# Last panel of the pooling output: latent rows first, context joins behind them, other banks and order at the heads' entry

## The chip, the cores and the metric

The kernel runs on one core of a Trainium2 chip. The metric is the device time of one execution, in microseconds: the median of three runs. Five engines work side by side, each on its own list of instructions in order: PE (matmuls), DVE (vector), ACT (activations), POOL (GpSimd) and SP, which here only issues DMAs. They meet at semaphores: an instruction waits until a counter has reached a value, and another engine's instruction raises it when it ends.

## The reference

Everything is float32. A first block (attention of three kinds and a feed-forward part with a short convolution) works on 256 tokens of width 2048. What the change touches lies in the second block, of two layers: a pooling layer on 256 latent and 256 context tokens, and a latent-attention layer (MLA) on both.

```python
for i in range(2):
    shift, scale, gate = jnp.split(jax.nn.silu(c) @ ada_w[i] + ada_b[i], 3, axis=-1)
    h_lat = rms_norm(x, pre_norm[i]) * (1 + scale[:, None]) + shift[:, None]
    shift_c, scale_c, gate_c = jnp.split(jax.nn.silu(c_ctx) @ ada_w[i] + ada_b[i], 3, axis=-1)
    h_ctx = rms_norm(ctx, pre_norm[i]) * (1 + scale_c) + shift_c
    if is_pool:      # i == 0
        y_lat = pool_branch(h_lat, ...)        # ends in (y * silu(gate)) @ pool_w_out
        y_ctx = pool_branch(h_ctx, ...)
    else:            # i == 1
        y_lat, y_ctx = mla_branch(h_lat, h_ctx, ...)    # begins with proj = h @ mla_w_in
    x = x + gate[:, None] * rms_norm(y_lat, post_norm[i])
    if i == 0:
        ctx = ctx + gate_c * rms_norm(y_ctx, post_norm[i])
```

So between the last matmul of `pool_w_out` and the first of `mla_w_in` lie, for the latent rows, the RMS norm of the output, the residual sum, a second RMS norm with scale and shift, and a transpose. The MLA layer then projects to low-rank queries and keys (`c_q`, `c_kv`), a rotary key part `k_r` and gates, and works on 16 heads.

## The kernel before

**Weights as a stream.** All weights pass through a ring of four slots (`RING`). One chunk is 256 rows of 512 (MLA input: 448) columns. SP loads it into `raw` (helper `load_chunk`), ACT rounds it to `hi` (L541, in `his`), DVE makes `lo = raw - hi` (L545, in `los`), and PE multiplies in three passes, hi x hi, hi x lo, lo x hi (`by_tokens`, L598), so that products keep nearly float32 precision. A slot of `raw` is free for the next load once its `lo` is made (`lo_split`), and `hi`/`lo` of a slot are free once PE has used them (`chunks_used`). SP, ACT, DVE and PE all walk the same list of chunks in order. In that list stand, between the weights, chunks of `ada_w` (adaLN weights of the second block), which DVE alone consumes: four multiply-adds on 128x512 (L568, L574). After eight such chunks PE turns the finished row into columns with 16 one-column matmuls (`turn_ada`, L647) and DVE takes them into `adat` (`take_ada`, L653). Where they stand is set by lists of numbers (`POOL_OUT_ORDER`, `MLA_IN_ORDER`).

**Pooling output.** `y` (512 tokens) times `pool_w_out`, in four panels of 512 columns, two to a turn (`pool_out_turn` on PE). A panel has eight chunks; each makes 24 matmuls: 2 row blocks x 4 token tiles (tiles 0 and 1 latent, 2 and 3 context, `TT = 2`, `NT = 4`) x 3 passes. Panels use PSUM banks 0-3 and 4-7 in turn. After a panel ACT squares each bank with a running sum (`yout_squares`, L1350), DVE multiplies each with the gates (`yout_gated`, L1706). After the last panel come the mean (`yout_mean_square`), a POOL power to -0.5 (`yout_roots`, L1087), and `yout_join` (L1722): residual plus normalised row, for the latent rows into `xres`, for the context rows into `yout`.

**Norm for the MLA layer.** Two `Norm` objects, `n_mla` for the latent and `n_mla_ctx` for the context rows: squares on ACT (`norm_squares`, L673), mean on DVE (L749), power on POOL (`norm_root`, L754), scaling on DVE (`norm_apply`, L759, into `xn4b`), then eight groups: four transposes on PE (`norm_turn`, L775, banks 4-7), scale and shift on ACT (`norm_hi`, L805), high and low part on DVE (`norm_shift_split`, L830 and L837) into `k4_hi` and `k4_lo`.

**MLA panels.** Seven panels of 448 columns in the order 0, 3, 1, 2, 4, 5, 6 (`MLA_ORDER`); "panel p" below counts in this order. Each has eight chunks of 12 matmuls for the latent tiles, in banks 0-1 or 2-3 by turns; panels 2 and 3 also compute context columns. The latent groups are turned among the first chunks of panel 0, the context groups among those of panel 1, and panel 2 needs all of the context's groups. ACT copies each finished panel to `proj_l` (L1397, `mla_taken`). Under panels 4 to 6 run the norms of `c_q` and `c_kv` and the rotary keys, turned into banks 4 and 5 (`kr_hi` on ACT, L1392; `kr_lo` on DVE, L1909).

**Heads.** Eight pairs of heads. Per pair: queries from two chunks (banks 0-1), keys (banks 2-3, L2296), turning of q (L2307, L2309), values (banks 2-3, L2319, copied by DVE to `v_sb`, L1868), scores (banks 4-7, L2330 and L2332), DVE's maxima, ACT's exponentials (L1416), transposes of the probabilities (L2339), rows (L2347). The first pair's queries to values stand ahead of the loop, with the transposing of the gate gains (`turn_gates`, L2226) before them; the silu of the gates (L1428) stands on ACT before the first exponential.

## Time and profile before

| | us |
|---|---|
| median of 3 runs | 2441.76 |
| lowest, highest run | 2439.11, 2446.45 |
| the profiled execution | 2439.29 |
| its span in the trace | 2437.5 |
| PE busy | 2336.4 (96%) |
| DVE busy | 1656.9 (68%) |
| ACT busy | 1041.2 (43%) |
| POOL busy | 76.2 (3%) |

The profiled execution is one run of its own; its trace starts and ends a little inside the measured time. Times "at 1896" are microseconds from the start of the span. A timeline row gives start, duration, engine, source line and instruction with its tiles; "x4" means four merged instructions, and square brackets hold the engine's idle time before it and what ended it. The clock is PE's, as a share of its full rate. An engine's share of busy time says little by itself: what counts is which wait ended last at a place where PE stood still.

### The profile page before, as it was taken

What the parts mean: (1) busy time and instruction counts of PE and PEld (TensorE: products, weight loads), DVE (VectorE), ACT (ScalarE), POOL (GpSimd) and SP (SyncE); (2) the same over time, 40 slices, a digit from 0 to 9 for tenths busy, and PEclk for the clock granted to TensorE, in tenths of its full rate; (3) what the DMA queues carried; (4) which work ended last, traced back from release to release, by engine and by line L of the source; (5) the groups of instructions that cost most, each with busy time, mean ns of one, the idle gap of its engine ahead of it and who ended that gap; (6) DMA issues with size and microseconds to landing.
All of it is one profiled execution on the core that took longest, in us unless ns stands there. A gap on an engine that the chain in (4) does not pass through costs nothing.

```text
span 2437.5 us, 32050 instructions
## 1 busy us (share of the span) xinstructions
PE 2336.4 (96%) x11221; PEld 1935.8 (79%) x11221; DVE 1656.9 (68%) x2401; ACT 1041.2 (43%) x1490; POOL 76.2 (3%) x112
## 2 busy tenths in 40 slices
PE   8999999999999999999969999999999699899997
PEld 6778778878877877778858888887788699799976
DVE  5378866687787786777748585756758666456544
ACT  5575654555555555333342222222222535443433
POOL 1022210000000000000000000000000000000000
PEclk9999999999999999999989999999999899999999
DMA  7956545666676766777735464645557256312243
GB/s 240 206 167 197 165 137 158 189 217 219 209 234 199 232 212 201 249 238 243 249 108 185 144 198 137 200 139 171 205 169 221 82 170 181 114 61 68 74 140 136
DMA packets 225516, 430.32 MB, mean 177 GB/s; under 512 B 13800, under 2 KB 38624, under 8 KB 224129
## 3 DMA queue, kind: packets, MB, share of 16 engines
q1 hardware_dynamic: 222112, 418.96, 55.2%
q10 hardware_dynamic: 2720, 9.83, 1.3%
q8 instruction: 63, 1.03, 0.2%
q14 instruction: 45, 0.36, 0.1%
q0 software_dynamic: 576, 0.14, 0.0%
HBM read 426.16 MB, written 2.72 MB: 176 GB/s over the span
## 4 chain that ended last, share of the span: by engine, by line
PE 63%; issue 19%; DVE 7%; DMA 6%; ACT 4%; DVEq 0%; POOL 0%; ACTq 0%; SPq 0%; POOLq 0%
PE ps L598 37%; PE ps L631 11%; PE ps L608 9%; DMA raw<-in_w_down 4%; DVE lo L545 2%; ACT hi L541 2%; DVE ada_acc L574 2%; PE ps L647 1%; DVE ustage L1630 1%; DMA raw<-in_w_in 1%; PE ps L2202 1%; PE ps L2127 0%; DMA poolm<-const_pool 0%; PE ps L1979 0%; PE ps L775 0%
## 5 line engine op out<-in xcount | busy, mean ns | idle before, releaser
L541 ACT ACTIVATE hi<-raw 128x1024 fp32r<-128x1024 f32 x604 | 635.3, 1059 | 1148.8 <-PE ps L598 536.2
L545 DVE TENSOR_TENSOR lo<-raw,hi 128x1024 fp32r<-128x1024 f32 x604 | 731.4, 1222 | 520.4 <-ACT hi L541 517.5
L574 DVE SCALAR_TENSOR_TENSOR ada_acc<-raw,csil,ada_acc 128x512 f32<-128x512 f32 x720 | 491.8, 746 | 2.5 <-DMA raw<-in_ada_w 2.3
L598 PE MATMUL ps<-hi,h_hi 128*128 128x512 f32 x960 | 383.2, 399 | 8.1 <-DVE lo L545 6.5
L598 PE MATMUL ps<-hi,h_lo 128*128 128x512 f32 x960 | 378.9, 395 | 0.0
L598 PE MATMUL ps<-lo,h_hi 128*128 128x512 f32 x960 | 378.7, 395 | 0.0
L598 PEld LDWEIGHTS ps<-hi,h_hi 128*128 128x128 f32 x960 | 180.8, 188 | 55.4 <-DVE lo L545 13.4
L598 PEld LDWEIGHTS ps<-hi,h_lo 128*128 128x128 f32 x960 | 180.7, 188 | 42.5
L598 PEld LDWEIGHTS ps<-lo,h_hi 128*128 128x128 f32 x960 | 180.9, 188 | 40.1
L598 PE MATMUL ps<-hi,g_hi 128*128 128x512 f32 x352 | 140.9, 400 | 6.6 <-DVE lo L545 6.3
L631 PE MATMUL ps<-hi,h_hi 128*128 128x512 f32 (+1 forms) x352 | 142.2, 404 | 2.9 <-DVE h_lo L736 2.9
L598 PE MATMUL ps<-lo,g_hi 128*128 128x512 f32 x352 | 139.1, 395 | 0.0
L598 PE MATMUL ps<-hi,g_lo 128*128 128x512 f32 x352 | 139.0, 395 | 0.0
L631 PE MATMUL ps<-hi,h_lo 128*128 128x512 f32 (+1 forms) x352 | 136.9, 389 | 0.0
L631 PE MATMUL ps<-lo,h_hi 128*128 128x512 f32 (+1 forms) x352 | 136.6, 388 | 0.0
L598 PE MATMUL ps<-hi,k_hi 128*128 128x448 f32 (+2 forms) x288 | 102.6, 356 | 1.1 <-DVE k_lo L837 0.6
L598 PE MATMUL ps<-hi,y_hi 128*128 128x512 f32 x256 | 102.6, 401 | 0.0
L608 PE MATMUL ps<-h_hi,hi 128*128 128x512 f32 x256 | 102.0, 398 | 0.0
L598 PE MATMUL ps<-hi,y_lo 128*128 128x512 f32 x256 | 101.9, 398 | 0.0
L598 PE MATMUL ps<-lo,y_hi 128*128 128x512 f32 x256 | 101.9, 398 | 0.0
L598 PE MATMUL ps<-hi,k_lo 128*128 128x448 f32 (+2 forms) x288 | 101.5, 353 | 0.0
L598 PE MATMUL ps<-lo,k_hi 128*128 128x448 f32 (+2 forms) x288 | 101.5, 352 | 0.0
(320 smaller groups left out, 3710.3 us busy)
## 6 DMA issues: line engine op xcount, KB each, us to landing
raw<-in_ada_w SPq DMA_DIRECT2D x192, 512.0 KB, 4.2
raw<-in_w_up SPq DMA_DIRECT2D x176, 512.0 KB, 4.5
raw<-in_w_down SPq DMA_DIRECT2D x88, 512.0 KB, 5.4
raw<-in_w_in SPq DMA_DIRECT2D x84, 512.0 KB, 4.5
raw<-in_pool_w_in SPq DMA_DIRECT2D x64, 512.0 KB, 4.1
raw<-in_mla_w_in SPq DMA_DIRECT2D x56, 448.0 KB, 4.1
raw<-in_w_out SPq DMA_DIRECT2D x32, 512.0 KB, 3.8
raw<-in_pool_w_out SPq DMA_DIRECT2D x32, 512.0 KB, 4.7
```

What stands on the lines that cost most here:

```text
L541: act.activation(hi[:, slot, :, :], raw[:, slot, :, :], ACT.Copy).then_inc(hi_split, 1 + ada)
L545: dve.tensor_tensor(lo[:, slot, :, :], raw[:, slot, :, :], hi[:, slot, :, :].bitcast(F32), ALU.subtract).then_inc(lo_split, 1)
L574: ins = dve.scalar_tensor_tensor(acc, raw[:, slot, k, :], csil[:, v, kt:kt + 1], acc, ALU.mult, ALU.add)
L598: mm = pe.matmul(ps[:, bank, 0:n], a[:, kt0 + k, tok * P:(tok + 1) * P], w[:, slot, k, col0:col0 + n], start=first and k == 0 and s == 0, ...
L608: mm = pe.matmul(ps[:, bank0 + n, :], w[:, slot, k, n * P:(n + 1) * P], a[:, kt0 + k, :], start=first and k == 0 and s == 0, stop=last and ...
L631: mm = pe.matmul(ps[:, PAIR * half + tok, 0:width], x, w[:, k, :], start=first and k == 0 and s == 0, stop=last and k == nk - 1 and s == 2)
L647: mm = pe.matmul(ps[:, bank, at:at + 1], acc, negones[:, 0:1], start=True, stop=True)
L1630: ins = dve.scalar_tensor_tensor(conv[which][:, m, back:SEQ], turned_u(m)[:, 0:SEQ - back], cols[:, bass.ds(ch + vec[0] * P + vec[1], 1)], ...
L2202: mm = pe.matmul(ps[:, m, s * SEQ + c0:(s + 1) * SEQ], u[:, TT * s + k, m * P:(m + 1) * P], poolm[:, bass.ds(n, 1), k, c0:].rearrange("p a ...
```

## The change

- **Pooling output.** The loop over the two turns is written out, each turn with its own list (`POOL_OUT_ORDERS`). The second turn carries one adaLN panel instead of two. In its last panel the first four chunks run as before for all four tiles; the last four run for tiles 0 and 1 alone, signal `lat_summed`, and then run again for tiles 2 and 3, which frees the slots.
- **Latent chain.** ACT squares and DVE gates tiles 0 and 1 alone; mean and power are made for these two; the latent rows are joined and normed. The splits of the first four MLA chunks stand one by one between the steps. The context's squares, products, mean, power and joins stand behind the latent groups, among splits of MLA chunks.
- **Norm.** `k4_hi` and `k4_lo` are tiles for latent and context apart. The latent groups turn in banks 4, 5, 0, 1; the squares are written to SBUF. The context groups turn at chunks 3 to 5 of panel 1 (before: 0 to 2).
- **MLA panels.** They start in banks 2-3 instead of 0-1. Two adaLN panels lie among their weights (16 chunks behind weights 15 to 35) instead of one (8 chunks behind 16 to 30).
- **Heads' entry.** The first queries need only the sixth copy of `proj_l`; `turn_gates` stands behind them; the first values go to banks 6-7; `kr_lo` and the gate gains are made in the last MLA panel; the first scores stand ahead of the loop, and each turn of the loop ends with the next pair's scores.

On DVE at the end of the pooling output, before the change (`yout` products, then mean and joins; `lo<-raw,hi` is a chunk's split):

```order
L653 TENSOR_SCALAR adat<-ps 128x8 [waits ada_turned]
L545 TENSOR_TENSOR lo<-raw,hi 128x1024 [waits hi_split]
L1706 TENSOR_TENSOR yout<-ps,gate_rows 128x512 [waits yout_squared0] x4
L1714 TENSOR_REDUCE ss<-panel_sums 128x4 [waits yout_squared0]
L1716 TENSOR_SCALAR ms<-ss 128x4 [waits yout_summed0]
L545 TENSOR_TENSOR lo<-raw,hi 128x1024 [waits hi_split]
L1683 TENSOR_TENSOR adat<-adat,cols 128x64 [waits ada_taken]
L1687 SCALAR_TENSOR_TENSOR hscale<-adat,cols 128x16 [waits ada_biased]
L1687 SCALAR_TENSOR_TENSOR hscale<-adat,cols 128x16
L1722 SCALAR_TENSOR_TENSOR xres<-yout,rstd,xres 128x2048 [waits yout_root0,yout_taken] x2
L1722 SCALAR_TENSOR_TENSOR yout<-yout,rstd,ctx_res 128x2048 [waits yout_root0,yout_taken,ctx_again]
L749 TENSOR_SCALAR ms<-ss 128x2 [waits norm_squared]
```

The same place on DVE after the change:

```order
L1714 TENSOR_TENSOR adat<-adat,cols 128x64 [waits ada_taken]
L1718 SCALAR_TENSOR_TENSOR hscale<-adat,cols 128x16 [waits ada_biased]
L1718 SCALAR_TENSOR_TENSOR hscale<-adat,cols 128x16
L1737 TENSOR_TENSOR yout<-ps,gate_rows 128x512 [waits yout_squared0] x2
L1745 TENSOR_REDUCE ss<-panel_sums 128x2 [waits yout_squared0]
L1747 TENSOR_SCALAR ms<-ss 128x2 [waits yout_summed0]
L1753 SCALAR_TENSOR_TENSOR xres<-yout,rstd,xres 128x2048 [waits yout_root0,yout_taken] x2
L549 TENSOR_TENSOR lo<-raw,hi 128x1024 [waits hi_split]
L761 TENSOR_SCALAR ms<-ss 128x2 [waits norm_squared]
L771 TENSOR_SCALAR xn4b<-xres,rstd 128x2048 [waits norm_root]
L771 TENSOR_SCALAR xn4b<-xres,rstd 128x2048
L549 TENSOR_TENSOR lo<-raw,hi 128x1024 [waits hi_split]
```

The scales moved ahead of the products, two products and both context joins left this place, and a split stands behind the joins and another behind the scaling.

On DVE at the heads' entry, before the change (`q_rope` is the last step of the rotary queries):

```order
L1854 TENSOR_TENSOR q_rope<-q_rope,q_swap 128x256 [waits q_swapped]
L545 TENSOR_TENSOR lo<-raw,hi 128x1024 [waits hi_split] x2
L1858 TENSOR_TENSOR kn_lo<-ps,kn_hi 128x1024 [waits kn_hi_done]
L1862 TENSOR_TENSOR qn_lo<-ps,qn_hi 128x512 [waits q_hi_done]
L1864 TENSOR_TENSOR qr_lo<-ps,qr_hi 128x256
L1868 COPY v_sb<-ps 128x1024 [waits chunks_used]
L545 TENSOR_TENSOR lo<-raw,hi 128x1024 [waits hi_split] x2
L1909 TENSOR_TENSOR kr_lo<-ps,kr_hi 128x1024 [waits kr_hi_done]
```

And in the last MLA panel on DVE after the change:

```order
L549 TENSOR_TENSOR lo<-raw,hi 128x1024 [waits hi_split] x5
L1881 TENSOR_TENSOR kr_lo<-ps,kr_hi 128x1024 [waits kr_hi_done]
L1726 TENSOR_TENSOR adat<-adat,cols 128x32 [waits ada_taken]
L1729 TENSOR_TENSOR hscale<-adat,cols 128x16 [waits ada_biased]
L1729 TENSOR_TENSOR hscale<-adat,cols 128x16
L549 TENSOR_TENSOR lo<-raw,hi 128x1024 [waits hi_split] x3
L1893 TENSOR_TENSOR q_swap<-ps,rope 128x4x16 [waits q_nope_ready,kr_turned]
```

`kr_lo` and the gate gains (`adat`, `hscale`) moved ahead of the last three splits of the MLA stream; before, `kr_lo` stood behind the copy of `v_sb` and two more splits.

The diff, cut to its core:

```diff
-POOL_OUT_ORDER = turn_order(2 * CH, evenly(2 * CH, 2 * CH))
+POOL_OUT_ORDERS = [turn_order(2 * CH, evenly(2 * CH, 2 * CH)), turn_order(2 * CH, [RING + 7 * m // CH for m in range(CH)])]
...
-MLA_PANELS, MLA_ADA = MLA_W // W_IN, 1
-MLA_IN_ORDER = turn_order(MLA_PANELS * CH, [2 * CH + 2 * m for m in range(CH)])
+MLA_PANELS, MLA_ADA = MLA_W // W_IN, 2
+MLA_IN_ORDER = turn_order(MLA_PANELS * CH, [2 * CH - 1 + 4 * m // 3 for m in range(2 * CH)])
...
-            yout_roots(0)
+            yout_roots(0, LAT)
             norm_root(pool, n_mla)
+            yout_roots(0, CTX)
             norm_root(pool, n_mla_ctx)
...
+                    if last:
+                        his(act, first, 0, 0, at + RING, end)
+                        act.wait_ge(lat_summed, 1)
+                        yout_squares(0, i * 2 + half, 4 * half, slice(0, TT))
...
+            his(act, C_MLA, 0, 0, 0, 1)
+            norm_squares(act, n_mla, lambda e, i: e.wait_ge(yout_added[0], i + 1), 0, lat_junk[:, :])
+            his(act, C_MLA, 0, 0, 1, 2)
             act.wait_ge(scales_ready, 4)
-            norm_hi(act, n_mla)
+            norm_hi(act, n_mla, {3: lambda: his(act, C_MLA, 0, 0, 2, 3), 5: lambda: his(act, C_MLA, 0, 0, 3, 4)})
+            yout_squares(0, D // W - 1, 4, slice(TT, NT))
...
             scales(1, V_PRE1)
-            for i in range(TT):
-                yout_join(0, i, xres[:, i, :], xres[:, i, :])
-            dve.wait_ge(ctx_again, 16)
-            yout_join(0, TT, yout[:, TT, :], ctx_res[:, 0, :])
+            yout_gated(0, D // W - 1, 4, slice(0, TT))
+            yout_mean_square(0, LAT)
+            for tok in range(TT):
+                yout_join(0, tok, xres[:, tok, :], xres[:, tok, :])
+            los(dve, C_MLA, 0, 0, 0, 1)
             norm_mean(dve, n_mla)
-            yout_join(0, TT + 1, yout[:, TT + 1, :], ctx_res[:, 1, :])
             norm_apply(dve, n_mla)
-            norm_shift_split(dve, n_mla)
+            los(dve, C_MLA, 0, 0, 1, 2)
+            norm_shift_split(dve, n_mla, {3: lambda: los(dve, C_MLA, 0, 0, 2, 3), 5: lambda: los(dve, C_MLA, 0, 0, 3, 4)})
...
             mla_los(0, 0, RING)
+            yout_gated(0, D // W - 1, 4, slice(TT, NT))
+            yout_mean_square(0, CTX)
+            dve.wait_ge(ctx_again, 16)
+            for m in range(TT):
+                mla_los(0, RING + m, RING + m + 1)
+                yout_join(0, TT + m, yout[:, TT + m, :], ctx_res[:, m, :])
+            mla_los(0, RING + TT, CH)
             norm_mean(dve, n_mla_ctx)
             norm_apply(dve, n_mla_ctx)
-            mla_los(0, RING, CH)
-            norm_shift_split(dve, n_mla_ctx)
+            mla_los(1, 0, 3)
+            norm_shift_split(dve, n_mla_ctx, {3: lambda: mla_los(1, 3, 4), 5: lambda: mla_los(1, 4, 5)})
...
-            mla_los(6, 0, CH)
+            mla_los(6, 0, RING + 1)
+            dve.wait_ge(kr_hi_done, 1)
+            dve.tensor_tensor(kr_lo[:, :, :], ps[:, 4:6, :], kr_hi[:, :, :].bitcast(F32), ALU.subtract).then_inc(kr_lo_done, 1)
             gate_gains(1, V_POST1)
+            mla_los(6, RING + 1, CH)
...
-            pair_v(0)
+            pair_v(0, 6)
             los(dve, C_HEADS, 0, 4, RING + 2, RING + 4)
-            dve.wait_ge(kr_hi_done, 1)
-            dve.tensor_tensor(kr_lo[:, :, :], ps[:, 4:6, :], kr_hi[:, :, :].bitcast(F32), ALU.subtract).then_inc(kr_lo_done, 1)
...
+                if last:
+                    for j in range(RING):
+                        before(CH + j)
+                        part(j, outs, True)
+                    for j in range(RING, CH):
+                        before(CH + j)
+                        mm = part(j, outs[0:TT], False)
+                    mm.then_inc(lat_summed, 1)
+                    for j in range(RING, CH):
+                        part(j, outs[TT:NT], True)
...
-                if p == 1:
-                    norm_ahead(pe, n_mla_ctx, j, False)
+                if p == 1 and j >= 3:
+                    norm_ahead(pe, n_mla_ctx, j - 3, False)
...
-                panel_by_tokens(pe, C_MLA, 0, MLA_IN_ORDER, p * CH, k4_hi, k4_lo, pair(p % 2) + ctx_too, W_IN,
+                panel_by_tokens(pe, C_MLA, 0, MLA_IN_ORDER, p * CH, k4_hi, k4_lo, pair(1 - p % 2) + ctx_too, W_IN,
...
+            pe.wait_ge(mla_taken, PAIR + len(MLA_ORDER) - 1)
+            pair_queries(0, C_HEADS, 0)
+            turn_gates(1, 7)
             pe.wait_ge(mla_taken, PAIR + len(MLA_ORDER))
-            turn_gates(1, 7)
-            pair_queries(0, C_HEADS, 0)
             pair_keys(0, 0)
             pair_keys(0, 1)
             pair_turn(0)
-            pair_values(0)
-            pe.wait_ge(gates_out, 2)
+            pair_values(0, 6)
             pe.wait_ge(kr_lo_done, 1)
+            pe.wait_ge(kn_lo_done, 1)
+            pair_scores(0, True)
+            pe.wait_ge(v_ready, FREE + 1)
             with pe.Fori(0, PAIRS - 1) as i:
-                pair_scores(i)
                 pair_queries(i + 1, C_HEADS + RING, i)
...
                 pair_columns(i)
-            pair_scores(PAIRS - 1)
+                pair_scores(i + 1)
```

## Rows read from the trace of the kernel before

**Rows 1.** Waits of PE, whole span: who waited for whom, total us, times, longest.

```profile
PE ps L775 <- DVE xn4b L759: 17.6, 2, 17.0
...
PE ps L598 <- DVE lo L545: 13.4, 21, 0.9
```

**Rows 2.** Timeline at the heads' entry: start, duration, engine, line, instruction; idle time before it.

```profile
2098.90 0.27 PE L2226 MATMUL ps<-ident,hscale 128*32 128x128 f32 x1 [2.95 <-DVE hscale L1698]
...
2112.97 0.39 PE L2319 MATMUL ps<-hi,ckv_hi 128*128 128x256 f32 x1 [1.72 <-DVE kn_lo L1858]
...
2120.94 3.69 ACT L1428 ACTIVATE proj_l<-proj_l 128x2048 f32<-128x2048 f32 x2
...
2122.39 1.22 DVE L1909 TENSOR_TENSOR kr_lo<-ps,kr_hi 128x1024 fp32r<-128x1024 f32 x1
...
2123.95 0.79 PE L2330 MATMUL ps<-kn_hi,qn_hi 128*128 128x512 f32 x1 [5.02 <-DVE kr_lo L1909]
...
2124.65 1.28 ACT L1416 ACT_TABLE_LOAD   x1
...
2132.28 0.34 PE L598 MATMUL ps<-hi,cq_hi 128*128 128x384 f32 x1
...
2136.49 1.03 PE L2339 MATMUL ps<-ident,mprobs 128*128 128x128 f32 x8
```

**Rows 3.** Timeline from the pooling output to the MLA panels, same columns.

```profile
1897.06 2.48 DVE L1706 TENSOR_TENSOR yout<-ps,gate_rows 128x512 f32<-128x512 f32 x4 [5.23 <-ACT yout L1350]
...
1899.74 1.22 DVE L545 TENSOR_TENSOR lo<-raw,hi 128x1024 fp32r<-128x1024 f32 x1
1899.90 1.93 POOL L1087 TENSOR_TENSOR rstd<-ms,halves 128x4 f32<-128x4 f32 x1 [658.22 <-DVE ms L1716]
...
1906.59 1.88 ACT L673 ACTIVATE ps<-xres 128x2048 f32<-128x2048 f32 x1 [0.26 <-DVE xres L1722]
...
1908.80 2.34 DVE L1722 SCALAR_TENSOR_TENSOR yout<-yout,rstd,ctx_res 128x2048 f32<-128x2048 f32 x1
1908.97 2.73 POOL L754 TENSOR_TENSOR rstd<-ms,halves 128x2 f32<-128x2 f32 x1 [7.15 <-DVE ms L749]
...
1918.32 0.47 PE L598 MATMUL ps<-hi,k_hi 128*128 128x448 f32 x1 [0.58 <-DVE k_lo L837]
```

**Rows 4.** Chain of waits, the end of PE's pooling output: start, duration, what.

```profile
1888.81 1.68 PE ps L647 x16
1890.49 5.70 PE ps L598 x24
```

**Rows 5.** Timeline of POOL: two powers with DVE waiting for them.

```profile
1231.17 0.69 POOL L754 TENSOR_TENSOR rstd<-ms,halves 128x2 f32<-128x2 f32 x1 [785.80 <-DVE ms L749]
...
1935.55 0.70 POOL L754 TENSOR_TENSOR rstd<-ms,halves 128x2 f32<-128x2 f32 x1 [23.84 <-DVE ms L749]
```

**Rows 6.** Stream in the MLA panels: timeline, a DMA group, windows as in rows 7.

```profile
1944.82 0.44 PE L775 MATMUL ps<-ident,xn4b 128*128 128x128 f32 x2 [0.71 <-DVE k_lo L837]
...
1967.57 2.73 DVE L574 SCALAR_TENSOR_TENSOR ada_acc<-raw,csil,ada_acc 128x512 f32<-128x512 f32 x4
...
2040.47 1.22 DVE L545 TENSOR_TENSOR lo<-raw,hi 128x1024 fp32r<-128x1024 f32 x1 [1.22 <-ACT hi L541]
...
raw<-in_mla_w_in SPq DMA_DIRECT2D x56, 448.0 KB, 4.1
...
1840.00:1860.00 20.00, 20.00 (x88) 16.24 (x87) 19.16 (x29) 5.49 (x11) 0.00 (x0) 1.00 0.64 206
...
1964.00:2032.00 68.00, 68.00 (x392) 64.87 (x392) 41.08 (x47) 19.54 (x19) 0.00 (x0) 1.00 0.59 171
```

**Rows 7.** Windows: length; busy PE, PEld, DVE, ACT, POOL; PE clock; DMA share, GB/s.

```profile
1901.00:1904.00 3.00, 0.00 (x0) 0.00 (x0) 2.42 (x4) 0.00 (x0) 0.82 (x1) 0.52 0.53 153
...
2099.00:2104.00 5.00, 5.00 (x21) 5.00 (x21) 0.00 (x0) 0.27 (x1) 0.00 (x0) 0.66 0.39 115
...
2124.00:2130.00 6.00, 6.00 (x15) 4.70 (x16) 1.38 (x3) 2.69 (x4) 0.00 (x0) 0.51 0.33 125
```

192 lines of the change are left out of this document (110 added, 82 removed).

## The prediction

> **What bounds the kernel now.** I read the list of PE's waits first. Its largest is one stop of 17.0 us before the transposes of `xn4b` [rows 1]: the place where the last panel of the pooling output ends and the MLA projection begins. The other place that I price is the entry to the heads, where three waits of 2.95, 1.72 and 5.02 us stand close together [rows 2]. Between the two PE runs nearly without a gap (68 of 68 us busy in panels 2 and 3 [rows 6]), so a microsecond taken from either is one of the total, as long as nothing new stops PE.
>
> In the timeline of the first place the reader should see one thread handed from engine to engine while PE has nothing: four products with the gates, a POOL power, joins of the two latent rows, the second row's squares, a POOL power again, then scaling and transposes, and only at 1918.32 the first matmul of the MLA panels [rows 3]. The chain view gives PE's last piece before it: 24 matmuls from 1890.49, 5.70 us, which end at 1896.19 [rows 4]. From work to work that is 22.1 us.
>
> **Part 1: the latent rows first.** The last four chunks now run for the two latent tiles, then again for the two context tiles. The matmuls stay 24 per chunk; half a chunk costs 5.70 / 2 = 2.85 us, so the latent sums are ready 4 x 2.85 = 11.4 us before PE is done. The second adaLN panel of this turn and its 16 transposing matmuls (1.68 us [rows 4]) leave the tail, which puts its end at 1894.5 and the latent sums at 1883.1. The 1.68 is paid again in MLA panel 4, and booked there.
>
> The thread gets shorter too. Two products with the gates instead of four: half of 2.48 us goes, 1.24 [rows 3]. The two POOL powers took 1.93 and 2.73 us, each while DVE ran an instruction on two SBUF tiles (the `lo` split at 1899.74, the context join at 1908.80 [rows 3]); where DVE only waited for it, the same power took 0.69 and 0.70 us, even after 785.80 us of idleness [rows 5]. In the new order DVE waits for both: the scales went ahead of them, the split between them, the context joins far behind. So I take 0.70 for each and save 1.23 + 2.03 = 3.26 us; the other end is nothing. Width could also explain the first power (128x4 there, 128x2 now), but not the second, which was 128x2 already.
>
> The Trainium skill, page "SBUF — State Buffer", section "Who interferes with whom", says that a DVE instruction with two SBUF inputs holds the port through which GpSimd reads, and that the later one is blocked. By that rule the 3.26 us go whole; by width alone only 1.23 would. The two powers beside a waiting DVE speak for the rule.
>
> The thread is then 22.1 - 1.2 - 3.3 = 17.6 us, and the first MLA matmul comes at 1883.1 + 17.6 = 1900.7 instead of 1918.3: **17.6 us earlier**. The `lo` splits that now stand inside the thread I cost at nothing: the one after the joins (1.22 us) lies beside ACT's second row of squares (1.88 us [rows 3]), the one after the scaling beside the transposes and ACT's first shift. If the cover is gone, each costs 1.22. The squares go to SBUF instead of PSUM; two other ACT passes over 128x2048 in SBUF take 3.69 us, 1.85 each [rows 2], so that is nothing too.
>
> **Part 2: what the MLA panels pay back.** Before, the first four MLA chunks were split ahead of the stop or in it. Now they stand in line on DVE among the norm's groups, and the context's products, mean, two joins (2.34 each [rows 3]), squares, scaling and shift fall into panels 0 and 1, while PE eats a chunk in 2.44 us (a split of 1.22 after 1.22 of waiting [rows 6]). I laid chunk after chunk out with these durations and a landing time of 4.1 us [rows 6]. PE waits in that layout: 0.4 and 0.3 before chunks 3 and 4 of panel 0; 1.9 before the context's transposes, now at chunk 3 of panel 1, since joins, a square of 2.1, a power and a scaling come late; 0.8 at the start of panel 2, where the rest of the context's `k_lo` and half an adaLN product stand ahead of the split; 1.8 and 0.8 in panel 4, where three of the moved adaLN chunks (2.73 us each [rows 6]) sit between weights that PE eats in 2.44. Together 6.0 us; the small waits for `k_lo` among the context's transposes (0.71 before [rows 6]) stay. With the moved transposes, 6.0 + 1.7 = 7.7. A landing of 5.5 us instead of 4.1 adds 3.5.
>
> PE still stops for 2.8 us before the first transpose. In the stop that began at 1896.19 the clock was down from about 1901 (0.52 over 1901 to 1904 [rows 7]), 4.8 us in, so I expect little: 0.5 for the chance of a half-speed start that costs up to 2. At the end of the MLA panels that leaves 17.6 - 7.7 - 0.5 = **9.4 us** gained, bounds 3 and 13.
>
> The eight adaLN chunks that moved: DVE was busy 41.08 of 68 us in panels 2 and 3 [rows 6]. Five more products fall there (13.7 us), 55 of 68, so I take them as hidden.
>
> **Part 3: the heads' entry.** (a) The MLA panels swap bank pairs, so the last one sits in banks 2 and 3, the first queries (banks 0 and 1) need no copy of it, and the gate gains are made earlier: the wait of 2.95 goes. (b) The first pair's values go to banks 6 and 7 and no longer wait for `kn_lo`: 1.72 goes. (c) `kr_lo` is made in the last panel, not behind the copy of V and two splits at 2122.39: 5.02 goes [rows 2]. (d) The stops cost clock: the granted clock (1.2 or 2.4 GHz) was 0.66 of full over 2099 to 2104 and 0.51 over 2124 to 2130, with PE busy in all of it [rows 7]. At half speed half of the time is lost, so 0.34 x 5 = 1.7 and 0.49 x 6 = 2.9 us. Sum 9.7 + 4.6 = **14.3 us**.
>
> What is late next: ACT's two silus (3.69 us) and the table load (1.28) before the first exponential [rows 2]. From the end of the MLA panels PE needs 22 us for queries, keys, turns, values and scores and 4.2 for the next queries (2132.28 to 2136.49 [rows 2]); it wants the second exponential at 26.4. ACT is freed by the values at 16.5, splits two chunks (2.0), ends the silus at 22.3 and the table load at 23.6, and the second exponential, held by DVE's maxima, at about 25.6. A margin of 0.8 us. `kr_lo` (1.22) in the last panel lies beside PE's 2.44 per chunk. The unrolled loops of SP and ACT and the contiguous `k4` tiles have no row; between -0.5 and +0.5, I take 0.
>
> **The sum.** 9.4 + 14.3 = 23.7 us. The profiled execution took 2439.29 us (span 2437.5), which makes 2415.6. It lies 2.5 us under the median of the runs shown, 2441.76; the same gain from the median is 2418.1. Forecast: **2418 us**.
>
> **Rivals.**
> - *The chunk stream falls behind (20 in 100).* A raw slot is freed by a split, and the splits now stand behind norm work. If loads land in 5.5 us or the context's thread is 3 us longer, the MLA part gains 3: 2424.5. For it: PE waited 21 times for `lo` even before [rows 1]. Against: DVE's spare time.
> - *Slow POOL powers and a fallen clock (8 in 100).* 3.3 + 1.5 us: 2423.
> - *The exponentials come late (6 in 100).* With ACT's line 5 us over PE's, the stop moves behind the scores and takes the clock along (2.9): 2426.
> - *The halves release nothing (2 in 100).* Were part of the latent chain still to wait for the context half, its 11.4 us stay and the gain is 12: 2429.5.
> - *Slower than before: DVE becomes the bound in the MLA panels (4 in 100).* Sixteen adaLN chunks of 2.73 us now stand between weights 15 and 35. Had PE to wait for all, 43.7 us: 2462. It decides from nine of them on (24.6 us, the whole gain). Against it: between 1840 and 1860 DVE was busy 19.16 of 20 us with such products and PE all of the 20 [rows 6]; PE's chunks were longer there, though.
>
> **How the numbers follow.** The forecast has 60 in 100. Its own bounds are gains of 28 (hardly a wait in panels 0 to 4) and 19. To leave out no more than 2 in 10 the range goes from there to the far end of the stream rival: 2411 to 2428. A measurement here tells 0.3%, 7.3 us, from no change. All cases but the last lie below 2434.4; I leave 5 in 100 for several of them at once and for a mild form of the last: faster 0.91, same 0.05, slower 0.04.
>
> **What would show it.** Right: PE idle about 3 us (not 17) before the first `xn4b` transposes; both powers of the latent thread near 0.7 us; the first MLA matmul some 6 us after the last pooling matmul; a wait of about 2 us for `xn4b` in panel 1; no wait over 1 us between the last MLA chunk and the first `mprobs` transposes, the clock at 1.00 throughout. Wrong: many waits of PE over 1 us for `lo` in panels 2 to 4, DVE above 90% there, a new wait for `mprobs` or `mnm`, or the clock at 0.5 in panel 0.

## The result, and the profile after

The changed kernel took **2420.9 us** (median of 4 runs, 2419.69 to 2425.15) against 2440.44 for the kernel before (4 runs): a ratio of 0.9924, 95% interval 0.9906 to 0.9943. A second series gave 2419.8 against 2436.77, 0.9934 (0.992 to 0.9948). So it is faster by 17 to 20 us, 0.7% to 0.8%. The forecast was 2418, range 2411 to 2428, a gain of 23.7. The profiled execution took 2421.59 us, 17.7 less than that of before. The time thus lies 3 us from the forecast and the gain 4 to 7 us below it: the kernel before, too, was faster in these series than the 2441.76 from which the forecast subtracts. Most of the change does what the forecast says, to within a microsecond; some 6 us are missing, all in one stage, and what took them was none of the rivals.

The waits of PE over the whole span (who waited for whom, total, times, longest) come first. The stop of 17 us before the transposes of `xn4b` [rows 1] is gone. The list has a line that the list of before had not, the wait for `adat L665`:

```profile
PE ps L608 <- DVE lo L549: 12.8, 18, 1.7
...
PE ps L659 <- DVE adat L665: 4.4, 1, 4.4
...
PE ps L787 <- DVE xn4b L771: 3.0, 4, 1.1
...
PE ps L608 <- DVE k_lo L851: 1.8, 1, 1.8
```

The thread from the pooling output to the MLA panels is the counterpart of [rows 3] and [rows 5]. First the chain view (start, duration, what), then the timeline (start, duration, engine, line, instruction, idle time before it):

```profile
1872.53 11.27 PE ps L608 x48
```

```profile
1884.55 1.29 DVE L1737 TENSOR_TENSOR yout<-ps,gate_rows 128x512 f32<-128x512 f32 x2 [10.78 <-ACT yout L1369]
...
1886.18 0.70 POOL L1105 TENSOR_TENSOR rstd<-ms,halves 128x2 f32<-128x2 f32 x1 [643.80 <-DVE ms L1747]
1886.99 4.62 DVE L1753 SCALAR_TENSOR_TENSOR xres<-yout,rstd,xres 128x2048 f32<-128x2048 f32 x2 [0.89 <-POOL rstd L1105]
1891.53 1.22 DVE L549 TENSOR_TENSOR lo<-raw,hi 128x1024 fp32r<-128x1024 f32 x1
...
1893.93 0.70 POOL L766 TENSOR_TENSOR rstd<-ms,halves 128x2 f32<-128x2 f32 x1 [7.05 <-DVE ms L761]
1896.09 0.30 PE L787 MATMUL ps<-ident,xn4b 128*128 128x128 f32 x1 [1.15 <-DVE xn4b L771]
1897.20 1.86 PE L787 MATMUL ps<-ident,xn4b 128*128 128x128 f32 x15 [0.81 <-DVE xn4b L771]
1900.89 0.48 PE L608 MATMUL ps<-hi,k_hi 128*128 128x448 f32 x1 [1.83 <-DVE k_lo L851]
```

The latent sums end at 1872.53 + 11.27 = 1883.80, PE's pooling output (its last matmul starts at 1894.55 and lasts 0.40) at 1894.95. Both powers take 0.70, and the first MLA matmul starts at 1900.89, 17.4 us earlier than the 1918.32 of [rows 3]. That is what was forecast (17.6). PE stands still for 1.15 us before the first transpose; 17 before, and about 3 forecast.

Then 14.5 of these 17.4 us are lost again by the end of the MLA panels: the transposes of `kr` (in the last of them) come at 2082.2, before at 2085.1. The timeline of PE in panel 4 shows where the largest part went:

```profile
2023.17 0.47 PE L608 MATMUL ps<-hi,k_hi 128*128 128x448 f32 x1 [1.55 <-DVE lo L549]
...
2037.11 0.37 PE L608 MATMUL ps<-hi,k_lo 128*128 128x448 f32 x1
2041.90 2.27 PE L659 MATMUL ps<-ident,ada_acc 128*128 128x1 f32 x10 [4.43 <-DVE adat L665]
```

L659 is the second of the two adaLN turns that the change puts into panel 4, and L665 is where DVE takes the result of the first. DVE's own timeline tells why it was late:

```profile
2033.26 0.17 DVE L761 TENSOR_SCALAR ms<-ss 128x2 f32<-128x2 f32 x1 [0.20 <-ACT ps L685]
2036.29 0.17 DVE L761 TENSOR_SCALAR ms<-ss 128x4 f32<-128x4 f32 x1 [2.85 <-ACT ps L685]
2036.36 0.88 DVE L771 TENSOR_SCALAR proj_l<-proj_l,rstd 128x512 f32<-128x512 f32 x2
2037.74 0.88 DVE L771 TENSOR_SCALAR proj_l<-proj_l,rstd 128x512 f32<-128x512 f32 x2 [0.50 <-POOL rstd L766]
2038.54 0.87 DVE L771 TENSOR_SCALAR proj_c<-proj_c,rstd 128x512 f32<-128x512 f32 x2
2039.33 2.35 DVE L549 TENSOR_TENSOR lo<-raw,hi 128x1024 fp32r<-128x1024 f32 x2
2041.60 0.15 DVE L665 TENSOR_SCALAR adat<-ps 128x8 f32<-128x8 f32 x1
```

The take of 0.15 us stands behind two means, of which the second waits 2.85 us for ACT's squares, three pairs of scalings and two splits. Before, the same line of work stood there and nobody waited for it, since there was one turn only. PE's wait for it is written into the helper: `turn_ada` waits until all earlier turns are taken (`ada_taken`), although the second turn here writes another bank (7, the first 6). Whether that wait could be dropped was not tried. The windows of this place (length; busy PE, PEld, DVE, ACT, POOL; granted PE clock; DMA share, GB/s) show the second cost, the clock. It went to half (1.2 of 2.4 GHz) at about 2040.3, while PE stood still, and came back only at about 2050.3:

```profile
2036.00:2041.00 5.00, 1.47 (x8) 1.00 (x6) 4.21 (x9) 3.10 (x5) 1.17 (x1) 0.93 0.11 43
2042.00:2050.00 8.00, 8.00 (x29) 7.48 (x30) 0.89 (x1) 0.00 (x0) 0.00 (x0) 0.50 0.50 166
```

From 2041.9 to 2050.3 PE worked at half speed, which costs 8.4 / 2 = 4.2 us. With the wait that is 4.4 + 4.2 = 8.6 us.

At the heads' entry none of the three waits of [rows 2] is left; PE had no idle time from 2083 to 2120, and the clock, which had fallen twice there [rows 7], stayed up:

```profile
2086.00:2100.00 14.00, 14.00 (x73) 12.82 (x72) 7.52 (x15) 7.05 (x9) 0.00 (x0) 1.00 0.51 169
2100.00:2120.00 20.00, 20.00 (x125) 18.35 (x124) 11.97 (x19) 12.84 (x19) 0.00 (x0) 1.00 0.30 93
```

The first `mprobs` transposes start at 2118.8, in the kernel before at 2136.5 [rows 2]. From the transposes of `kr` (2082.21, before 2085.13) to there it was 51.4 us and is 36.6, 14.7 less before rounding. Behind that point the length is the same: 301.0 us to the end of the span, 301.0 before.

### The profile page after: what moved, and what is told of

It is laid out like the page before. It is cut to its first block, busy times and chain, and to the rows that moved or that the text cites. A ratio compares the mean times of both kernels' runs of the same rounds, so it can differ in the third digit from the quotient of the medians.

```text
span 2419.8 us, 31795 instructions
## 1 busy us (share of the span) xinstructions
PE 2337.7 (97%) x11221; PEld 1935.9 (80%) x11221; DVE 1655.8 (68%) x2403; ACT 1040.7 (43%) x1490; POOL 73.1 (3%) x113
## 4 chain that ended last, share of the span: by engine, by line
PE 62%; issue 19%; DVE 8%; DMA 6%; ACT 4%; DVEq 0%; POOL 0%; ACTq 0%; SPq 0%; POOLq 0%
PE ps L608 37%; PE ps L643 10%; PE ps L620 9%; DMA raw<-in_w_down 3%; DVE lo L549 3%; ACT hi L545 2%; DVE ada_acc L578 2%; DMA raw<-in_w_in 1%; PE ps L659 1%; DVE ustage L1661 1%; PE ps L2244 1%; PE ps L2169 0%; DMA raw<-in_ada_w 0%; PE ps L2021 0%; PE ps L2020 0%
## 5 line engine op out<-in xcount | busy, mean ns | idle before, releaser
L608 PEld LDWEIGHTS ps<-hi,h_lo 128*128 128x128 f32 x960 | 181.5, 189 | 42.6
```

The lines of the kernel that those rows point to most:

```text
L608: mm = pe.matmul(ps[:, bank, 0:n], tokens(a, kt0 + k, tok), w[:, slot, k, col0:col0 + n], start=first and k == 0 and s == 0, stop=last and ...
```

## Experiments

The table below has every run made. Absolute times shift by up to 9 us from run to run in the part ahead of the change (the power of the first norm starts anywhere from 1227.2 to 1236.3), so I count between landmarks: P, the start of POOL's second power of the latent thread (`rstd`, 1893.93 above); M, the first MLA matmul; C, POOL's first power of the context thread; K, the transposes of `kr`; E, the first `mprobs` transposes. All in us, one profiled execution each; the last column is the ratio of the timed runs, where a kernel had more than one:

| kernel | P to M | P to C | P to K | K to E | ratio to before (95%) |
|---|---|---|---|---|---|
| before | | | | 51.4 | 1 |
| changed, first profile | 7.0 | 24.3 | 188.3 | 36.6 | 0.9924 (0.9906 to 0.9943) |
| x2b_after (the same program) | 7.0 | 26.1 | 190.0 | 36.6 | 0.9934 (0.992 to 0.9948) |
| x1_take | 7.0 | 26.2 | 181.5 | 36.6 | 0.9911 (0.9896 to 0.9927) |
| x6_fill | 7.0 | 24.3 | 179.6 | 36.6 | 0.990 (0.9885 to 0.9915) |
| x7_lofirst | 6.2 | 23.5 | 178.8 | 36.6 | 0.9898 (0.988 to 0.9916) |
| x8_spread | 7.0 | 26.2 | 186.8 | 36.6 | 0.9921 (0.9906 to 0.9936) |
| x2_norm | 7.0 | 26.0 | 189.8 | 49.6 | 0.9982 (0.997 to 0.9995) |
| x3_heads | | | | 36.6 | 0.9939 (0.9916 to 0.9962) |
| x4_whole | 7.3 | 24.7 | 188.3 | 36.6 | 0.9969 (0.9955 to 0.9983) |
| x5_power | 8.2 | 25.5 | 189.6 | 36.6 | one execution |
| x9_values | 7.0 | 24.4 | 188.5 | 38.6 | one execution |
| x10_krlo | 7.0 | 26.2 | 189.6 | 43.8 | one execution |
| x11_gates | 7.0 | 24.4 | 188.5 | 40.4 | one execution |

**The wait in panel 4: x1_take.**

```diff
             mla_los(4, 0, RING)
+            take_ada(dve, ADA_MLA, 6)
             norm_mean(dve, n_cq)
...
-            mla_los(4, RING, RING + 2)
-            take_ada(dve, ADA_MLA, 6)
-            mla_los(4, RING + 2, CH)
+            mla_los(4, RING, CH)
```

> The changed kernel with one line moved: DVE takes the first transposed adaLN panel right after the splits that belong to the first four chunks of panel 4, ahead of the two means and the scalings of c_q and c_kv; it stood behind them and two more splits. In the changed kernel PE waited 4.43 us for that take before the second turn, and the granted clock was 0.50 from about 2040.2 to 2050.3, with PE busy in nearly all of it. Theory: the wait and the low clock have this one cause. Both go: 4.4 + about 5 = 9.4 us, the time about 2412 (a ratio to before near 0.988), the clock 1.00 through panels 4 and 5, less up to 1.5 us of new short waits for lo. Rival 1, the clock fell for another reason (the many one-column transposes of the turns): only 4.4 us go, about 2416.5, and the clock still falls at the second turn. Rival 2, the stream is the bound there, and PE waits for lo in panel 5 instead: under 2 us go.

Measured: the take now runs at 2034.65, the second turn follows without a wait in 1.84 us, and PE is busy in all of the stretch at full clock:

```profile
2036.00:2052.00 16.00, 16.00 (x91) 14.89 (x91) 10.71 (x17) 10.15 (x17) 1.17 (x1) 1.00 0.62 193
```

P to K fell from 190.0 (x2b_after, which has the same slow start of panel 0, see below) to 181.5, by 8.5 us. From the wait of 1.55 us in panel 4, which both have, to K it is 8.7 us less than in the changed kernel. That is what 4.4 + 4.2 had said, and a little under the 9.4 expected. Both rivals fall: the clock did not drop at the turns themselves, and no new wait for `lo` came up behind. The timed gain is less clean. The median was 2416.78 us, not 2412; its ratio lies 1.3 to 2.3 thousandths (3 to 6 us) under those of the changed kernel, and the intervals overlap. In the profiled execution 1.8 us were lost in the tail (302.8 from E to the end instead of 301.0, with the clock at 0.83 over 2310 to 2320, where the two programs are equal). The other runs have no trace, and the runs of this kernel differ by 6 us among themselves.

**The changed kernel again: x2b_after.** In x1_take and x2_norm P to C had taken 26 us, in the changed kernel 24.3, at a place where the programs are equal.

> The changed kernel once more, for a comparison on the same chip with the kernels beside it. Theory: ratio to before near 0.992, as measured. The second look at its trace also tells whether the granted clock at the start of panel 0, 1.00 in its first profile and 0.50 for about 6 us in two of its variants (2 us later each at the context's thread), falls in this kernel too from one run to the next: then the time is up to 2 us longer and nothing in the program differs. Rival: the clock holds there in the changed kernel as a rule, and the variants differ for a reason of their own.

Measured: 26.1 us in the same program. Its clock fell at the start of panel 0, and its first profile's had not. Windows of x2b_after, whose first MLA matmul is at 1896.74, then of the first profile:

```profile
1890.00:1894.00 4.00, 2.03 (x13) 1.40 (x12) 3.49 (x3) 0.76 (x2) 0.48 (x1) 0.97 0.32 108
1894.00:1896.00 2.00, 1.86 (x9) 1.45 (x7) 0.90 (x3) 2.00 (x6) 0.00 (x0) 0.50 0.35 51
1896.00:1900.00 4.00, 3.26 (x9) 2.92 (x10) 2.65 (x6) 2.39 (x5) 0.00 (x0) 0.50 0.25 93
```

```profile
1896.00:1900.00 4.00, 2.16 (x16) 1.75 (x16) 2.90 (x4) 2.16 (x5) 0.00 (x0) 1.00 0.13 19
1900.00:1904.00 4.00, 3.11 (x17) 2.86 (x18) 2.80 (x6) 2.55 (x5) 0.00 (x0) 1.00 0.27 100
```

So a run of the same program gains or loses 1.8 us here. It also bounds what one profile can say: the 17.7 us between the two first profiles hold a full-clock panel 0 that other runs did not get.

**Keeping PE at work in the thread: x6_fill**, on top of x1_take.

```diff
+        def fill(pe, count):
+            for _ in range(count):
+                pe.transpose(ps[:, 3, 0:P], ident, ident)
...
                         if g == 0 and m == 0 and len(n.parts) == 1:
+                            if n is n_mla:
+                                fill(pe, (8, 5)[i])
                             pe.wait_ge(n.scaled, n.scaled0 + i + 1)
...
+                if (p, j) == (0, 0):
+                    norm_ahead(pe, n_mla, 0, False)
+                    fill(pe, 12)
                 if p == 0:
-                    norm_ahead(pe, n_mla, j)
+                    norm_ahead(pe, n_mla, j) if j else pe.wait_ge(n_mla.lo_done, n_mla.groups0 + -(-CK_T // n_mla.per))
```

> The kernel with the early take, and 25 transposes of the identity into bank 3, which nobody reads: 8 before the first transpose of xn4b, 5 between that and the second row's, 12 before the first MLA matmul, where PE was idle 1.17, 0.81 and 1.11 to 1.83 us. Theory: the granted clock falls because PE pauses there; with PE at work it stays at 1.00 from 1890 to 1914 and panel 0 runs at full speed: 2 us less than x1_take's profiled run in this stretch (the power of the context's thread 24 us behind that of the latent thread, not 25.5), 1 to 2 us in the median. Rival 1: the clock falls whatever PE does there, and nothing changes. Rival 2: the filling transposes come late and push the thread: 0.5 to 1.5 us slower.

Measured: full clock through the place, P to C 24.3 instead of 26.2, P to M unchanged. Windows of x6_fill, first MLA matmul at 1904.62:

```profile
1898.00:1904.00 6.00, 5.48 (x44) 4.68 (x42) 4.51 (x6) 2.76 (x7) 0.35 (x1) 1.00 0.33 94
1904.00:1910.00 6.00, 5.47 (x31) 4.99 (x31) 3.65 (x8) 4.46 (x8) 0.00 (x0) 1.00 0.15 56
```

The median is 2413.4 us, in the same series as the changed kernel's 2419.8, and the intervals do not overlap (0.9885 to 0.9915 against 0.992 to 0.9948). The early take and the filling together are worth some 6 us in the timed runs. By the landmarks it is more, 190.0 - 179.6 = 10.4 us from P to K; where the other 4 went is open, but in these two profiles it is ahead of P (1897.65 against 1889.78), where the programs are equal. That the filling holds the clock rests on two profiles, this one and x7_lofirst's. Without it there are eight with the same start of panel 0: in five the fall costs 1.8 us (P to C 26.0 to 26.2: x2b_after, x1_take, x2_norm, x8_spread, x10_krlo), in two it is short, lies within the transposes of `xn4b` and costs nothing (24.4: x9_values, x11_gates), in one it does not come. Two of two against one of eight speaks for the filling and does not prove it. x5_power and x4_whole, whose pauses at this place are longer, show the fall too, at 1899 and before the first transpose.

**The order of the first split: x7_lofirst**, on top of x6_fill with 7 transposes instead of 12 in the third gap.

```diff
             high(0)
             for g in range(n.groups):
-                if g + 1 < n.groups:
+                if g + 1 < n.groups and (g or not lo_first):
                     high(g + 1)
                 dve.wait_ge(n.hi_done, n.groups0 + g + 1)
...
+                if lo_first and not g:
+                    high(1)
```

> The kernel with the early take and the filling transposes (7 instead of 12 in the third gap), and for the latent rows DVE makes k_lo of the first group before k_hi of the second; before, the first k_lo waited 0.49 + 0.43 us for that. Theory: the first MLA matmul comes 0.9 us earlier, counted from the latent thread's second POOL power (7.0 to 6.1 us), and panel 0 goes on without a new wait: 0.9 us under x6_fill, whose ratio was 0.990. Rival: the next chunk waits for k_lo of a later group, and nothing is gained. The difference is at the edge of what five rounds tell; the trace decides.

Measured: P to M 6.2 instead of 7.0, and the 0.8 us are still there at C and at K. The median, 2413.52 us, does not show it; the ratio of 0.9898 (0.988 to 0.9916) is the lowest of all. It is the fastest version here, about 6 us under the changed kernel.

**Spreading the adaLN chunks: x8_spread**, on top of x1_take.

```diff
-MLA_IN_ORDER = turn_order(MLA_PANELS * CH, [2 * CH - 1 + 4 * m // 3 for m in range(2 * CH)])
+MLA_IN_ORDER = turn_order(MLA_PANELS * CH, [13 + 3 * m // 2 for m in range(2 * CH)])
```

> The kernel with the early take, and the 16 adaLN chunks of the MLA panels behind weights 13, 14, 16, 17 and so on to 35, two of every three weights, instead of three of every four from weight 15 on. Theory (three adaLN chunks close together hold the splits up, since they hold slots of the ring of four): the waits of 1.5 us in panel 4 and 0.4 us before it go, the gain is 1 to 2 us over x1_take. Rival (the chunks that now start in panel 1 meet the context's thread there, where DVE is busy): PE waits 1 to 3 us for lo or xn4b in panel 1 or 2, and the time is the same or worse.

Measured: the rival. The wait of 1.55 us in panel 4 became two of 0.23 and 1.07, but at the end of the context's thread PE stood for 3.19 us (timeline, then window), the clock fell behind it, and P to K is 5.4 us (before rounding) longer than x1_take's (a wait for `k_lo` before it grew as well, from 0.38 to 1.36):

```profile
1953.22 0.65 PE L608 MATMUL ps<-hi,k_hi 128*128 128x448 f32 x1 [3.19 <-DVE lo L549]
```

```profile
1953.00:1958.00 5.00, 4.78 (x16) 4.34 (x17) 5.00 (x8) 1.55 (x2) 0.00 (x0) 0.66 0.63 194
```

**POOL's power: x5_power.** The changed kernel with a split beside the second latent power.

```diff
-            los(dve, C_MLA, 0, 0, 0, 1)
             norm_mean(dve, n_mla)
+            los(dve, C_MLA, 0, 0, 0, 1)
```

> The changed kernel with the first lo split of the MLA chunks moved behind the latent rows' second mean, so that DVE subtracts two SBUF tiles (1.22 us) while POOL raises the two mean squares to the power; in the changed kernel DVE only waited there. Theory (POOL's power is held by a DVE instruction on two SBUF tiles): the power that took 0.70 takes 1.6 or more, as the one for the context rows did (1.61, beside such a split), xn4b is scaled about 1.0 us later, and the other latent power stays at 0.70. Rival (the long powers of before came from their width or from code that had to be loaded): it stays at 0.70 and xn4b comes only 0.4 us later, for the split's own length.

Measured:

```profile
1894.50 1.22 DVE L549 TENSOR_TENSOR lo<-raw,hi 128x1024 fp32r<-128x1024 f32 x1
...
1894.67 1.60 POOL L766 TENSOR_TENSOR rstd<-ms,halves 128x2 f32<-128x2 f32 x1 [7.04 <-DVE ms L761]
```

The power takes 1.60, the other one, which DVE waits for, 0.70 as ever, and the scaling comes 0.9 us later, counted from the first power. Same instruction, same width, same place; only its neighbour on DVE changed. In the three cases of a 128x2 power that starts just behind such an instruction it ends 0.55 or 0.56 us after that instruction: here (split until 1895.72, power until 1896.27), in the changed kernel (1919.31, 1919.86) and in the kernel before (join until 1911.14, power until 1911.70 [rows 3]). The rule of the Trainium skill that the prediction drew on (page "SBUF — State Buffer", section "Who interferes with whom") is borne out. The context's power in the changed kernel had shown it too: 1.61 us beside the split that starts at 1918.08.

Width has a share of its own, which the prediction left out. A power on 128x4 beside a DVE without two SBUF tiles stands in the trace of before, among the norms of `c_q` and `c_kv`:

```profile
2047.61 1.17 POOL L754 TENSOR_TENSOR rstd<-ms,halves 128x4 f32<-128x4 f32 x1 [2.33 <-DVE ms L749]
```

So of the 1.23 us that the first latent power lost (1.93 to 0.70) some 0.47 are its width (1.17 against 0.70) and 0.76 the split beside it.

**Latent rows first or chunk by chunk: x4_whole.** The changed kernel, the last four chunks not halved.

```diff
                     for j in range(RING, CH):
                         before(CH + j)
                         mm = part(j, outs[0:TT], False)
-                    mm.then_inc(lat_summed, 1)
-                    for j in range(RING, CH):
+                        if j == CH - 1:
+                            mm.then_inc(lat_summed, 1)
                         part(j, outs[TT:NT], True)
```

> The changed kernel, but in the last four chunks of the pooling output each chunk runs for its latent and then its context tiles, as before, instead of all latent ones first. Norm order, splits and the moved adaLN panel stay. Theory (the latent thread hangs on the latent sums alone): those end 2.85 us before PE's last pooling matmul instead of 11.4, so the first MLA matmul comes about 8.2 us later than the changed kernel's (1909 instead of 1900.9) with PE idle some 9 us before the first transposes; of this panels 0 to 2 give back about 2 (the waits of 0.5, 1.0 and 0.4 us for the stream and the context), and the fallen clock costs up to 2: about 8 us over the changed kernel, 2429. Rival 1, the stream or the 4.4 us wait in panel 4 sets the time behind it: the loss is given back by then, 0 to 3 us over. Rival 2, the halves release nothing: no difference at all.

Measured: 0.9969 against the 0.9934 of x2b_after and the 0.9924 of the first series, 3.5 and 4.5 thousandths or 8.5 and 11 us slower; 8 were expected. PE stood for 9.53 us before the first transpose instead of 1.15, 8.4 us more, and P to K is the same 188.3 as in the changed kernel: nothing is given back later. That halving changes the time was only argued before; here it is shown, with its size.

**Each stage alone: x2_norm and x3_heads.** x2_norm is the changed kernel with the old heads' entry, x3_heads the kernel before with the new one and the swapped bank pairs. The edit that is undone in one and made in the other, cut:

```diff
-            mla_los(6, 0, CH)
+            mla_los(6, 0, RING + 1)
+            dve.wait_ge(kr_hi_done, 1)
+            dve.tensor_tensor(kr_lo[:, :, :], ps[:, 4:6, :], kr_hi[:, :, :].bitcast(F32), ALU.subtract).then_inc(kr_lo_done, 1)
...
-            pe.wait_ge(mla_taken, PAIR + len(MLA_ORDER))
-            turn_gates(1, 7)
+            pe.wait_ge(mla_taken, PAIR + len(MLA_ORDER) - 1)
             pair_queries(0, C_HEADS, 0)
+            turn_gates(1, 7)
+            pe.wait_ge(mla_taken, PAIR + len(MLA_ORDER))
...
-            pair_values(0)
+            pair_values(0, 6)
```

> The changed kernel with the heads' entry of before: gates turned and the first queries only after the last panel is copied, values in banks 2 and 3 behind kn_lo, kr_lo behind the copy of V and two splits, scores at the head of the loop. The latent rows first, the moved adaLN panel and the swapped bank pairs stay. Theory (the parts are separate and add up): its gain over before is what the changed kernel had gained at the transposes of kr, about 3 us: 2437, ratio near 0.999; three waits near 3, 1.7 and 5 us stand again at the entry. Rival, the entry's gain depended on the norm's part, or the other way round: the gain is over 6 us or below 0.

> The kernel before with only the new heads' entry (and the swapped bank pairs of the MLA panels that it needs). Theory: the entry alone brings 14.7 us as read from the traces (17.7 earlier at the first mprobs transposes, of which 2.9 were there at the transposes of kr): about 2425.5, ratio 0.994, no wait over 1 us from the last MLA chunk to the first mprobs transposes, clock 1.00. Rival: ACT's silus or the exponentials, which had slack when the norm's part ran earlier, become late: a wait for mprobs of 2 to 5 us and only 10 to 12 us gained.

Measured: x2_norm 0.9982, a gain of 4.4 us (1.2 to 7.3 by the interval), x3_heads 0.9939, 14.9 us. Together 7.9 thousandths against 6.6 and 7.6 for both at once: they add up, within what the intervals tell. From K to E x3_heads has the changed kernel's 36.6. x2_norm has 49.6 and not 51.4: behind the wait of 2.95 us its clock stayed at 1.00 (2097 to 2102), where in the kernel before it was 0.66 [rows 7]. So the 1.7 us of clock behind that wait do not come in every run. The waits of PE at the entry of x2_norm are the three of [rows 2] again, to the tenth:

```profile
PE ps L2390 <- DVE kr_lo L1950: 5.0, 1, 5.0
...
PE ps L2267 <- DVE hscale L1729: 3.0, 1, 3.0
...
PE ps L2377 <- DVE kn_lo L1899: 1.7, 1, 1.7
```

x3_heads has none, PE busy 22.00 of 22 us from 2100 to 2122 at full clock. So the exponentials are in time also where the part before the entry is late.

**The three edits of the entry, undone one by one: x9_values, x10_krlo, x11_gates.** Each is the changed kernel with one edit taken back, in this order: the values (with the copy of V that follows them), `kr_lo`, the gates.

```diff
-            pair_values(0, 6)
+            pair_values(0)
+            pe.wait_ge(gates_out, 2)
```

```diff
-            mla_los(6, 0, RING + 1)
-            dve.wait_ge(kr_hi_done, 1)
-            dve.tensor_tensor(kr_lo[:, :, :], ps[:, 4:6, :], kr_hi[:, :, :].bitcast(F32), ALU.subtract).then_inc(kr_lo_done, 1)
+            mla_los(6, 0, CH)
...
             pair_v(0, 6)
             los(dve, C_HEADS, 0, 4, RING + 2, RING + 4)
+            dve.wait_ge(kr_hi_done, 1)
+            dve.tensor_tensor(kr_lo[:, :, :], ps[:, 4:6, :], kr_hi[:, :, :].bitcast(F32), ALU.subtract).then_inc(kr_lo_done, 1)
```

```diff
-            pe.wait_ge(mla_taken, PAIR + len(MLA_ORDER) - 1)
+            pe.wait_ge(mla_taken, PAIR + len(MLA_ORDER))
+            turn_gates(1, 7)
             pair_queries(0, C_HEADS, 0)
-            turn_gates(1, 7)
-            pe.wait_ge(mla_taken, PAIR + len(MLA_ORDER))
```

> The changed kernel with the first pair's values in banks 2 and 3 again, behind kn_lo, and the wait for gates_out behind them; the rest of the new entry stays. In the changed kernel 36.6 us lie between the transposes of kr and the first mprobs transposes, in the kernel before 51.4. Theory: the wait of 1.72 us for kn_lo stands again, with little of the clock: 38.3 to 39.5 between those two points. Rival: the values' place also carried the 5 us wait, since the copy of V and what follows on DVE come later: over 41.

> The changed kernel with kr_lo made where it was made before, behind the copy of V and two splits, instead of in the last MLA panel. Theory: PE waits about 5 us for kr_lo before the scores, and the clock is near 0.5 for some 6 us behind it: 36.6 + 5 + 2.9 = 44.5 us between the transposes of kr and the first mprobs transposes. Rival: the copy of V comes earlier in this order than in the kernel before, the wait is under 3 us and the clock holds: under 40.

> The changed kernel with the old head of the entry: PE waits for the copy of the last panel, turns the gates and only then runs the first queries; kr_lo and the values stay at their new places. Theory: the wait of 2.95 us for the gate gains stands again and the clock is down for some us behind it (1.7): 36.6 + 2.95 + 1.7 = 41.2 us between the transposes of kr and the first mprobs transposes. Rival: the wait comes back but is made good behind it, since ACT and DVE have 3 us more for the silus and the exponentials: under 38.5.

Measured, K to E against 36.6: x9_values +2.0 (a wait of 1.72, full clock behind it), x10_krlo +7.2 (a wait of 4.74, then the clock at 0.56), x11_gates +3.8 (a wait of 2.01, then 0.66). The windows behind the waits of x10_krlo and of x11_gates:

```profile
2117.00:2123.00 6.00, 5.42 (x14) 4.33 (x15) 1.58 (x4) 3.61 (x4) 0.00 (x0) 0.56 0.46 161
```

```profile
2095.00:2100.00 5.00, 4.67 (x18) 4.68 (x19) 0.72 (x1) 0.54 (x2) 0.00 (x0) 0.66 0.64 196
```

Each is within a microsecond of its expectation. In x11_gates the wait is 2.01 instead of 2.95 and for the copy, not for the gate gains, because those are still made early; I had overlooked that. In sum 12.9 of the 14.7 us (before rounding); the other 1.8 were not separated.

## Why the prediction was right where it was, and where it failed

**The thread: right.** Predicted 17.6 us from the latent sums to the first MLA matmul, measured 1900.89 - 1883.80 = 17.1. The sums were predicted 11.4 us before PE's end and came 11.1 before it. The gate products took 1.29 instead of 2.48, both powers 0.70 and not 1.93 and 2.73. x5_power shows why for the second; of the first's 1.23 us about 0.47 are width, so the prediction's account of it is right only in part, and its sum is right because both causes went. The splits inside the thread cost nothing where they were put; x5_power moves one by a single line, and the scaling comes 0.9 us later, the first MLA matmul 1.2. x4_whole confirms the size of the whole idea (8.5 to 11 us for 8).

The sign "PE idle about 3 us" failed: it was 1.15. The 2.8 of the prediction does not follow from its own terms, which give 17.0 - 1.2 - 3.3 - 11.4 = 1.1 (the stop of before, less the savings in the thread and the earlier sums). The 1.68 of the moved turn, which takes the end of the sums and the end of PE's work forward alike, was added once more.

**The payback in the MLA panels: one term missing.** From M to K the kernel before needed 2085.1 - 1918.3 = 166.8 us. The forecast added 7.7 for waits and the moved turn and 0.5 for the clock, so 175.0; measured were 2082.2 - 1900.9 = 181.3. Singly: 0.52 for the stream in panel 0 (0.4 and 0.3 forecast), 0.17 + 0.87 for `xn4b` (1.9), 0.42 at panel 2 (0.8), 1.55 in panel 4 (1.8 and 0.8). DVE was busy 53.9 of 67 us over 1949 to 2016 (55 of 68 forecast). The layout of the stream was thus right and a little too dark: without the wait for the take, in x6_fill, M to K takes 2077.26 - 1904.62 = 172.6, only 5.8 over before.

The step that failed is the sentence "The 1.68 is paid again in MLA panel 4, and booked there". I booked the matmuls of the moved turn and not what they wait for. A turn waits until DVE has taken the previous one. The second turn stands two chunks (some 5 us) behind the first, and between them DVE has a line with a wait for ACT in it, 8.3 us from 2033.26 to the take at 2041.60. Cost: 4.4 us of wait and 4.2 us of half clock, 8.6 together, shown by x1_take (8.5 to 8.7). All of it could have been read ahead: the order of DVE's instructions was known, and the means and scalings of `c_q` and `c_kv` stand in the trace of before, with the same 2.85 us of waiting for ACT. I had laid out DVE only for the splits of the chunk stream. None of the rivals named it either; "the stream falls behind" has the right size by accident and the wrong cause.

So at the end of the MLA panels 2.9 us were gained and not 9.4, just under the prediction's own lower bound of 3. The gap of 6.5 is the missing term (181.3 - 172.6 = 8.7 from M to K), less 2.4 by which the other payback was over-booked (8.2 for 5.8), plus 0.2 by which the first matmul came later than forecast (17.4 earlier, not 17.6).

These figures compare with one profile of the kernel before, whose clock was back at 1918.1, just as panel 0 began. In x3_heads, which is that kernel up to the last panel but for the swapped banks, it came back only at about 1920.9, and M to K took 169.1 us instead of 166.8. The gain at K is thus uncertain by some 2 us on the side of before as well.

**The clock in panel 0: risk named, price too thin.** A "clock at 0.5 in panel 0" was a sign of being wrong, and x2b_after, the same program, shows it. I put in 0.5 for "the chance of a half-speed start that costs up to 2". It costs 1.8 us, and did so in five of the eight profiles that share this start of panel 0, which would make the term 1.8 x 5/8 = 1.1. In the first profile it cost nothing, so it has no part in the 6 us.

**The heads' entry: right.** Predicted 14.3, measured 2136.49 - 2085.13 = 51.36 less 2118.83 - 2082.21 = 36.62, 14.7. (a) wait and clock 4.6 predicted, 3.8 when undone alone; (b) 1.7 and 2.0; (c) with its clock 7.9 and 7.2. Of the 14.7 us, 1.7 hang on the clock that had fallen behind the first wait in the profile of before and had not in x2_norm: from there the gain would be 13.0. The margin for the second exponential was put at 0.8 us (its terms, 22 + 4.2, give 26.2 and not 26.4, so 0.6); it ends at 2117.7, 1.1 us before the first transposes of `mprobs` at 2118.8, and no wait for it appeared in any run.

**The sum.** 2.92 + 14.74 = 17.66 us, the difference of the two profiled executions (17.7). The forecast of 23.7 was 6 us too much against them, and 4.2 and 6.7 too much against the medians of the two series. A gain of 17.7 lies outside the forecast's own bounds (19 to 28); the time fell into the range through the slack that was there for another rival, the stream. That is luck in part.

## What to carry to other kernels

When a piece of work is moved or doubled, write down for each of its instructions what it waits for, and lay the releasing engine's whole queue out up to that point, with its own waits for third engines; a result of 0.15 us that stands behind such a wait can hold PE for 4.4. Price a stop of PE with the clock behind it: here it nearly doubled the cost of one stop (4.4 + 4.2 us) and added half to another (4.7 + 2.5 in x10_krlo). Where the order of a tail may be chosen, run first the rows on which a long thread across engines hangs; the rest is then its cover.

## What the runs showed of the hardware

- The granted clock fell at the start of panel 0 although no single pause of PE ahead of it was over 1.2 us: in x2b_after it fell at about 1893.9, behind pauses of 1.17 and 0.81 with one transpose between them. In the first profile of the same program, with pauses of 1.15, 0.81 and 1.83 at the same place, it did not fall (seven of eight profiles with this start show a fall). With transposes of the identity in the pauses (0.20, 0.32 and 0.53 left) it held in two of two profiles. I had expected a small risk, not the rule.
- A wait of 1.72 us (x9_values) left the clock alone, one of 2.95 us at the heads' entry left it alone in x2_norm and was followed by 0.66 over 5 us in the kernel before, one of 2.01 us at another place (x11_gates) was followed by 0.66 over 5 us, one of 3.19 (x8_spread) by 0.66, one of 4.74 (x10_krlo) by 0.56 over 6 us, one of 4.43 by 0.50 over 8 us. The length of a stop alone does not tell whether the clock falls.
- A DVE split of 1.22 us that starts 0.17 us ahead of it turns a POOL power of 0.70 us into one of 1.60; the power ends 0.55 us after the split. Alone, the same power takes 0.70 us on 128x2 and 1.17 us on 128x4.
